# Gathering tokens for the experts: one fp32 product replaced by two fp32r products of high and low parts

## What is computed

```
def moe_swiglu(x, router, wg, wu, wd):
    logits = (x @ router).astype(jnp.float32)
    top_v, top_i = lax.top_k(logits, TOP_K)
    w = jax.nn.softmax(top_v, axis=-1)
    comb = jnp.einsum('blk,blke->ble', w, jax.nn.one_hot(top_i, N_EXPERTS, dtype=jnp.float32)).astype(x.dtype)
    y = jnp.zeros_like(x)
    for e in range(N_EXPERTS):
        y = y + comb[..., e:e + 1] * swiglu(x, wg[e], wu[e], wd[e])
    return y
```

## Time and profile before

| what | value |
|---|---|
| median of 3 runs | 2626.25 us (2621.33 to 2628.59) |
| the profiled execution | 2624.61 us, of which 2622.8 us lie between its first and last instruction |
| PE busy | 2425.3 us, 92% of the span |
| PE weight loads (PEld) busy | 2093.5 us, 80% |
| DVE busy | 1634.3 us, 62% |
| ACT busy | 1074.9 us, 41% |
| mean granted TensorE clock | 0.933 |

### The profile page before, as it was taken

How to read it: one execution, slowest core, us unless ns; L and a number is a source line. 1 busy time by engine, 2 the same in 40 slices (tenths; PEclk the granted TensorE clock), 3 DMA queues, 4 the chain that set the end, 5 groups by cost and what they waited for, 6 DMA issues and landing times.

```text
span 2622.8 us, 38245 instructions
## 1 busy us (share of the span) xinstructions
PE 2425.3 (92%) x14436; PEld 2093.5 (80%) x14436; DVE 1634.3 (62%) x2112; ACT 1074.9 (41%) x1450; POOL 178.0 (7%) x247
## 2 busy tenths in 40 slices
PE   7899988999999998899799998899999999999996
PEld 6878868876899888789688867687877878778786
DVE  4553853653565454455744733688787877878776
ACT  3322411321333343223222220566675756666663
POOL 0211111201000001111011110000000000000000
PEclk8998988898999999888898988799999999999998
DMA  5323411222444342333110421798888988889871
GB/s 192 106 79 130 139 57 41 100 98 79 145 162 165 119 155 90 101 121 124 66 65 33 140 75 51 279 338 283 302 315 300 331 298 315 298 298 335 292 277 66
DMA packets 122566, 456.43 MB, mean 174 GB/s; under 512 B 14056, under 2 KB 14474, under 8 KB 120018
## 3 DMA queue, kind: packets, MB, share of 16 engines
q1 hardware_dynamic: 118818, 432.66, 46.7%
q0 software_dynamic: 3632, 22.12, 2.3%
HBM read 443.72 MB, written 11.00 MB: 173 GB/s over the span
## 4 chain that ended last, share of the span: by engine, by line
PE 74%; DVE 15%; issue 6%; ACT 3%; POOL 1%; DVEq 0%; DMA 0%; SPq 0%; ACTq 0%; POOLq 0%
PE ps L720 7%; PE ps L721 7%; PE ps L722 7%; PE ps L767 5%; DVE weights_low L2249 4%; PE ps L1287 4%; PE ps L1289 4%; PE ps L1288 4%; PE ps L1309 3%; PE ps L1310 3%; PE ps L1311 3%; PE ps L1260 3%; PE ps L761 2%; PE ps L802 1%; PE ps L913 1%
## 5 line engine op out<-in xcount | busy, mean ns | idle before, releaser
L720 PE MATMUL ps<-u_high,tiles_high 128*128 128x288 f32 x1688 | 531.5, 315 | 6.0 <-DVE tiles_low L1712 6.0
L721 PE MATMUL ps<-u_low,tiles_high 128*128 128x288 f32 x1688 | 518.5, 307 | 0.0
L722 PE MATMUL ps<-u_high,tiles_low 128*128 128x288 f32 x1688 | 516.5, 306 | 0.0
L1712 DVE TENSOR_TENSOR tiles_low<-ring,tiles_high 128x1024 fp32r<-128x1024 f32 x238 | 292.7, 1232 | 216.0 <-ACT tiles_high L1368 214.6
L720 PEld LDWEIGHTS ps<-u_high,tiles_high 128*128 128x128 f32 x1688 | 337.7, 200 | 15.8 <-issue 12.0
L721 PEld LDWEIGHTS ps<-u_low,tiles_high 128*128 128x128 f32 x1688 | 337.6, 200 | 0.6
L2249 DVE TENSOR_TENSOR weights_low<-expert_ring,weights_high 128x1024 fp32r<-128x1024 f32 x288 | 334.5, 1220 | 5.0 <-ACT weights_high L1621 2.0
L722 PEld LDWEIGHTS ps<-u_high,tiles_low 128*128 128x128 f32 x1688 | 337.7, 200 | 0.0
L1368 ACT ACTIVATE tiles_high<-ring 128x1024 fp32r<-128x1024 f32 x238 | 250.5, 1053 | 172.8 <-DMA ring<-in_stream 82.9
L1287 PE MATMUL ps<-weights_high,u_high 128*128 128x512 f32 (+1 forms) x768 | 297.5, 387 | 23.1 <-DVE weights_low L2249 22.4
L2249 DVE TENSOR_TENSOR weights_low<-ring,weights_high 128x1024 fp32r<-128x1024 f32 x240 | 280.2, 1218 | 43.2 <-ACT weights_high L1621 42.0
(11 more groups left out here) (381 smaller groups left out, 3315.1 us busy)
## 6 DMA issues: line engine op xcount, KB each, us to landing
ring<-in_stream SPq DMA_DIRECT2D x530, 512.0 KB, 4.2
expert_ring<-in_stream SPq DMA_DIRECT2D x288, 512.0 KB, 5.6
arena<-in_state POOLq DMA_DIRECT2D x8, 1024.0 KB, 5.1
state_s<-arena POOLq DMA_DIRECT2D x8, 1024.0 KB, 4.2
const<-in_const SPq DMA_DIRECT2D x1, 2052.5 KB, 12.1
arena<-in_const POOLq DMA_DIRECT2D x2, 832.0 KB, 5.1
h<-in_x SPq DMA_DIRECT2D x1, 1152.0 KB, 5.3
y<-acc POOLq DMA_DIRECT2D x1, 1152.0 KB, 4.4
```

Source lines behind the costliest of these rows:

```text
L720: mm(out, hi[k], uh[:, k, :], start=k == 0, stop=False)
L721: mm(out, hi[k], ul[:, k, :], start=False, stop=False)
L722: last = mm(out, lo[k], uh[:, k, :], start=False, stop=k == KD - 1)
L1712: tt(t_low[:, q % HELD, :], ring[:, (t % RING) * TILE:(t % RING + 1) * TILE], t_high[:, q % HELD, :].bitcast(F32), ALU.subtract).then_inc( ...
```

## The change

The tokens are no longer kept as one fp32 matrix. ACT writes `utok_high` in fp32r (same three instructions, other target). DVE makes the low part, in six new instructions, in memory that is free at that time: the first two are 128x1024, the last four are 32x256, each of these four followed by a wait on its own semaphore. `gath` becomes fp32r; it holds only zeros and ones, so it needs no low part. The gather has two fp32r products, high and low, where it had one fp32 product.

```diff
+        hot_t, uth_t = sb("hot", 3 * PLACES, F32R), sb("tokens_high", 3 * D_MODEL, F32R)
+        gath = hot_t[:, :].rearrange("p (b c) -> p b c", b=3)
+        utok_high = uth_t[:, :].rearrange("p (b c) -> p b c", b=3)
...
-        gath, gathw = [e_carve(3 * PLACES).rearrange("p (b c) -> p b c", b=3) for _ in range(2)]
+        gathw = e_carve(3 * PLACES).rearrange("p (b c) -> p b c", b=3)
...
-        utok = e_carve(3 * D_MODEL).rearrange("p (b c) -> p b c", b=3)
+        low_parts = [(uh_t, KD * PLACES, 1024), (ul_t, KD * PLACES, 1024)] + [
+            (x, at0, 256) for x, at0 in ((uh_t, 2048), (ul_t, 2048), (th_t, NF * PLACES), (tl_t, NF * PLACES))]
+
+        def utok_low(b, f):
+            x, at0, n = low_parts[b if b < 2 else 2 + f // 256]
+            o = at0 + f % n
+            return x[:, o:o + P]
...
                         for k in range(KD):
                             for b, (t0, nt) in enumerate(TB):
-                                last = mm(bank(k // 4)[:, PLACES * (k % 4):PLACES * (k % 4 + 1)], utok[0:nt, b, P * k:P * k + P],
-                                          gath[0:nt, b, :], start=b == 0, stop=b == 2)
+                                out = bank(k // 4)[:, PLACES * (k % 4):PLACES * (k % 4 + 1)]
+                                mm(out, utok_high[0:nt, b, P * k:P * k + P], gath[0:nt, b, :], start=b == 0, stop=False)
+                                last = mm(out, utok_low(b, P * k)[0:nt], gath[0:nt, b, :], start=False, stop=b == 2)
...
                 tt(nrt, cnt[:, 0:1], cnt[:, 1:2], ALU.add).then_inc(rounds_ready, 1)
+                for b in range(2):
+                    x, at0, n = low_parts[b]
+                    tt(x[:, at0:at0 + n].rearrange("p (g c) -> p g c", g=2), ps_t[:, M + 1 + 2 * b:M + 3 + 2 * b, :],
+                       utok_high[:, b, :].rearrange("p (g c) -> p g c", g=2).bitcast(F32), ALU.subtract)
+                for g in range(4):
+                    x, at0, n = low_parts[2 + g]
+                    tt(x[0:32, at0:at0 + n], bank((M + 5 + g // 2) % 8)[0:32, n * (g % 2):n * (g % 2) + n],
+                       utok_high[0:32, 2, n * g:n * g + n].bitcast(F32), ALU.subtract).then_inc(dve_step, 1)
+                    dve.wait_ge(dve_step, steps.next())
                 V.memset(ps_t[:, M + 4:M + 6, :], 0.0)
```

More of the change, by code:

```diff
@@ L560, in build @@
         xg_high, xg_low = [x[:, 0:KD * PLACES].rearrange("p (k c) -> p k c", k=KD) for x in (uh_t, ul_t)]
-        e_cols = REGION - 2 * SPLITS * TILE - (ERING - RING) * TILE
+        hot_t, uth_t = sb("hot", 3 * PLACES, F32R), sb("tokens_high", 3 * D_MODEL, F32R)
+        gath = hot_t[:, :].rearrange("p (b c) -> p b c", b=3)
+        utok_high = uth_t[:, :].rearrange("p (b c) -> p b c", b=3)
+        e_cols = REGION - 2 * SPLITS * TILE - (ERING - RING) * TILE - 3 * PLACES - 3 * D_MODEL
         e_mem = sb("expert_memory", e_cols)
@@ L1596, in experts @@
                 act.wait_ge(utok_ps, 1)
-                A(utok[:, 0:2, :].rearrange("p b (g c) -> p (b g) c", g=2), ps_t[:, M + 1:M + 5, :], ACT.Copy).then_inc(scat_ready, 1)
-                A(utok[0:32, 2, 0:512], bank(M + 5)[0:32, :], ACT.Copy)
-                A(utok[0:32, 2, 512:1024], bank(0)[0:32, :], ACT.Copy).then_inc(expw_ready, 1)
+                A(utok_high[:, 0:2, :].rearrange("p b (g c) -> p (b g) c", g=2), ps_t[:, M + 1:M + 5, :], ACT.Copy).then_inc(scat_ready, 1)
+                A(utok_high[0:32, 2, 0:512], bank(M + 5)[0:32, :], ACT.Copy)
+                A(utok_high[0:32, 2, 512:1024], bank(0)[0:32, :], ACT.Copy).then_inc(expw_ready, 1)
                 act.wait_ge(sel_ready, 1)
@@ L2289, in experts @@
                         for b, (t0, nt) in enumerate(TB):
-                            last = tt(gathw[0:nt, b, :], gath[0:nt, b, :], wts[0:nt, b, bass.ds(e, 1)].to_broadcast([nt, PLACES]), ALU.mult)
+                            last = tt(gathw[0:nt, b, :], gath[0:nt, b, :].bitcast(F32), wts[0:nt, b, bass.ds(e, 1)].to_broadcast([nt, PLACES]), ALU.mult)
                         last.then_inc(gath_ready, 1)
```

## The result

The changed kernel takes 2652.75 us (median, 2649.1 to 2658.9) against 2623.79 for the kernel before, run beside it: a ratio of 1.0115, 95% interval 1.0097 to 1.0134. That is about 30 us slower, where 13 were forecast, and the time lies above the range.

What follows compares the result with a forecast made beforehand. PE, busy for 92% of the span, was taken to bound the kernel. First gather -3.4, subtractions +4.2, seven later gathers -12 and the clock's falls +24 made +13 us: 2639 us, range 2613 to 2650.

Steps and rivals of the forecast that it cites:

- The side: Whole kernel: slower, by 0.5%; slower (above 2634.1 us) had a chance of 0.54.
- the mechanism: Seven later gathers: too little streaming between weight loads makes the clock fall near their end, returning in or after the scatter.
- term of seven iterations: Later iterations: 1.7 us gained in the gather against 3.4 lost with the clock, each 1.7 longer, 12 in all.
- Block at full clock: One of the gather's eight blocks: 1.05 us falls to 0.83, so a gather takes 6.7 us, 1.7 less.
- the bare ones fall from 0.205 to 0.15: Four steps per gather block whose weight load isn't hidden: load plus stream, fp32r halving the streaming; sizes in us.
- Price of a fall: Gather and scatter per later iteration: 2.1 us in the scatter plus 1.3 in the gather's end, 3.4 together.
- The tail: Gather's end at half clock: two of eight blocks at 1.46 instead of 0.83 us, 1.3 us more.
- First gather: First iteration, at half clock: streaming falls, 3.4 us less, so the gather takes 11.7 us.
- Subtractions: Six DVE instructions before the loop, uncovered: 4.2 us more, PE's idle time 7.1 instead of 2.89.
- Covered steps of 0.11: Two steps per gather block where streaming hides under loading 128 columns of weights: they stay at 0.11 us.
- the clock holds: Rival, chance 0.20: the clock holds in every gather, 11 us less, 2615 us.
- fp32r of 128 columns costs what fp32 does: Rival, chance 0.12: gather stays at 8.40 us, clock at 1.00, only the subtractions are left, 2630 us.

Runs made afterwards that it cites:

- narrow_fp32: The kernel before, still fp32, with each of the 48 gather records streaming 64 instead of 128 columns: 2646.22 us, ratio 1.0101.
- subs_only: The kernel before with only the six subtractions added, their results unused and its gather untouched: 2629.54 us, ratio 1.0011.
- dense_fill: The changed kernel with one unused fp32r product of 512 columns behind each block of the gather: 2653 to 2682 us, ratio 1.0183.
- high_only: The changed kernel without the low product, so 24 records in a gather instead of 48: 2616.75 us, ratio 0.9957.

## Why the prediction was wrong, step by step

The side was right and so was the mechanism: the clock falls in each of the seven gathers, near their end, though PE never pauses, and the scatter pays for it. narrow_fp32 shows the cause by itself. The Trainium skill (TensorE: Matmul & The Clock Gate, Why this matters for your kernels) would have the clock hold here, since there is no idle gap; the fall after 4.86 us in which PE was busy for 4.86 speaks against that as the only way to lose it. Two sizes failed, both in the same term of seven iterations, and both made the change look better than it is.

- **Block at full clock: 0.83 forecast, 0.954 measured; a gather 7.5 instead of 6.7.** The failing step is "the bare ones fall from 0.205 to 0.15". It took the whole excess of all four bare steps as streaming that fp32r halves. Only the two between records of equal rows fell, to 0.16; the two at which the rows change, 128 to 32 and back, stayed at 0.20. They do so in narrow_fp32 too, at 64 columns of fp32, so what bounds them isn't the streaming; in the changed kernel the loads at these places start 0.26 us apart instead of 0.11. The seven gathers gave back 0.80 us each at full clock, 5.6 in all, not 12: 6.4 us of the miss.
- **Price of a fall: 3.4 forecast, 4.7 measured.** The tail was three blocks, not two: 9.54 - 7.53 = 2.0 instead of 1.3, or 0.67 for each block, where 0.63 was forecast. The scatter was taken from the first iteration as +2.1, where the clock came back 4.15 us after the gather; here the low stretch began three blocks before the scatter and ended with it, so it paid 2.7. Seven falls cost 33.1 us, not 24: 9.1 us of the miss.
- **First gather: 3.4 less forecast, 1.7 measured,** at half clock throughout, where the block's streaming was again overrated; its scatter gave 0.55 of it back, so 1.15: 2.3 us of the miss.
- **Subtractions: +4.2 forecast, +4.0 measured;** PE's idle time 7.1 forecast, 6.88 measured. Right, and subs_only shows them alone.
- **Covered steps of 0.11:** right, for fp32r at 128 columns, for fp32 at 64, and for all 48 records of a padded gather. What these have in common is the load of 128 columns of weights, and in the timeline of PEld the loads start 0.11 apart.

The misses add up to 6.4 + 9.1 + 2.3 - 0.2 = 17.6 us, and 30.4 less the 12.8 that the forecast's terms make is 17.6.

Of the rivals, "the clock holds" and "fp32r of 128 columns costs what fp32 does" fell with the trace; the second comes true in the padded form, 5.30 against 5.36. The Trainium skill (FP8 and Floating Point Precision, TensorE Precision Notes) states the four passes of a true fp32 product; the single pass of a reduced one is the prediction's own reading, and the gather didn't halve: it went from 8.33 to 7.53 us at full clock. The forecast's range for itself ended at 2650, since it allowed the fall to come two blocks earlier but held the block's 0.83 for certain, although it came from widths of 384 and 512.

Open is what decides whether the clock falls in one iteration and not in the next, and for how long: the first differs between iterations of the same code in dense_fill, the second also in high_only. The runs don't tell.

## What to carry to other kernels

When a matmul's step is set by its weight load, halving what streams saves nearly nothing, and it can cost the clock, here 4.7 us for 0.8 gained in each iteration; before thinning such products, look for records in the trace that are as thin, and price the dense work behind them at half clock too. Look at the steps inside a block first: the records next to a block of fewer rows cost up to twice the others, and zeros in the missing rows removed 3 us of 8.3 from each gather, which no change of type did. Work that is done once still counts in full where one engine is ahead of all others, and the place for it is in a wait of that engine: there the subtractions cost 2.8 us less than behind it.

## What was unexpected in the hardware

- A change of rows between records (128 to 32 or back) costs a step of 0.20 to 0.21 us at full clock whatever is streamed: fp32 at 128 columns, fp32 at 64, fp32r at 128; with a single short record between full ones (high_only) it was 0.25 on the way back. Steps between full rows are 0.11, but the one between the two short records, and the one right behind a change back, are 0.16, and 0.21 with fp32 at 128 columns.
- 128 rows instead of 32 don't only cost nothing: the padded fp32 gather raised the clock from 0.50 within its first 8.33 us (mean 0.66), where the old one stayed at 0.50 for 15.05. In fp32r, with the same padding, it stayed at 0.50 through the first gather's 10.30 us.
- The granted clock fell while PE was busy without a pause, in every one of the seven later iterations of the changed kernel, of narrow_fp32 and of high_only, and in five of seven of dense_fill, in the gather or in the scatter right behind it. In the changed kernel it stayed low for 10.2 us, far into the dense scatter, and only then came back.
